# HGRN2 levels: q and k scaled in place by running products of the decays, in place of cumulated logarithms, differences and exponentials

## Chip, core and metric

The kernel runs on one core of one Trainium2 chip. The metric is device time in microseconds (us) of one execution, as the median of several runs. The engines are TensorE (PE; PEld is its weight load), VectorE (DVE), ScalarE (ACT), GpSimd (POOL) and SyncE (SP, which issues the weight DMAs).

## What is computed

Three blocks run over 256 tokens with a model width of 1024: a convolution and gated-delta layer, an HGRN2 layer, and a second block of attention heads and an MLP. The change lies in the HGRN2 layer, of 16 heads of width 128:

```
f = lower_bound + (1 - lower_bound) * sigmoid(f_raw);  q = silu(q_raw);  k = 1 - f
S_t = diag(f_t) S_{t-1} + k_t v_t^T;   o_t = S_t^T q_t
```

Written out, o_t is a sum over s <= t of v_s times the dot product of q_t and k_s, each channel weighted by the product of f over (s, t]. That product is what the change computes in another way.

## The kernel before

**Staging.** All tensors lie with the channel on the partition and the tokens along the free axis. The 16 heads are done in four groups g of HG = 4 heads, so q, k and f of a group are 128 x 1024 elements each (4 heads x 256 tokens). Weights come as slabs of 128 x 2048 words into a ring of six buffers RAW. ACT rounds each slab to WH (L1355; a ring of three), DVE writes the remainder WL (L1783): the steps `split:k:i`. ACT may start split k once PE has used slab k-3. Each projection of the odd layer is one slab, done by PE in two halves, `first:name` and `name`: f, q1 and z1 with 24 matmuls of 256 columns per half, the values i with 12 of 512 columns per half. Slabs 50 to 53 are f:1:0, f:1:1, z1:0:0, z1:0:1; 58 and 59 are f:2:0 and f:2:1; 60 to 63 are z1:1:0, z1:1:1, q1:2:0, q1:2:1; 66 and 67 are f:3:0 and f:3:1; 74 to 78 are z1:3:0, z1:3:1 and the first three of out:1.

**The levels.** Within a chunk of 128 tokens, the pairs (s, t) are divided into NL = 7 levels by the block size s = 1, 2, 4, ..., 64: at a level, t lies in the second half of a block of 2s tokens and s in its first half. For each group:

- `hf` takes the logarithm of f (ACT L1578) and cumulates it along the tokens (DVE L2060, eight scans).
- `hx(i)` subtracts from the cumulated logarithms the value at the middle of each block (DVE L2087, 1024 elements), and takes exponentials of both halves (ACT L1586, L1587).
- `hy(i)` multiplies q's second halves and k's first halves by them into a tile HX of two halves, one for even and one for odd i (DVE L2104, L2105, 512 elements each).
- `hd` and `hm(i)` are 8 matmuls of 128 x 128 each on PE (16 instructions in the trace, "PS<-layer ... x16"): `hd` is k against q as they are, `hm(i)` is HX against itself.
- `hd` on DVE masks the diagonal into HA (L2069), `hp(i)` copies the entries of level i into HA (L2110).
- `hc` is the product between the two chunks, `ho` the output against the values, `hr` the root mean square: two wide matmuls on PE, the root on ACT (L1365, L1366, L1371), and five operations on DVE (L1750 to L1752, L1794, L1795). `hr(g)` reads the banks that `hm(g+1, 0)` writes, and `hm(g+1, 0)` waits for it.

**Order.** Every engine runs its steps in an order written out by hand (ORDER_T for PE, ORDER_S for ACT, ORDER_V for DVE), one after the other, each waiting on semaphores for what it needs. On PE the projections stand between the `hm` steps. ACT loads another table whenever the function set changes (L1718). Before the change, `hy(i)` waits for `hm(i-2)` (the same half of HX). In the stretch at group 2 DVE's order before is `hy:2:0 hx:2:2 split:66:73 hz:1 hr:1:0 split:67:74 hy:2:1 hy:2:2 hd:2 hx:2:3`.

Of the kernel before, what the change touches and what calls it, by code (L numbers as in the profile page):

```python
# [487 lines left out]
gu:1:4:1 gu:1:5:0 gp:1:5:1 gp:1:6:0 gu:1:5:1 gu:1:6:0 gp:1:6:1 gv:1:0 gu:1:6:1 gs:1 gks:1 gv:1:1 go:1 gr:1:0 gr:1:1
pl:0:0 first:out:0:0:3 first:out:0:1:3 out:0:0:3 out:0:1:3 xt:0:0:0 pl:0:1 xt:0:0:1 ada:0:0 ada:0:1 ada:1:0 ada:1:1
xt:0:1:0 adat:0 first:gate:0:0:0 xt:0:1:1 first:gate:0:0:1 gate:0:0:0 gate:0:0:1 first:gate:0:1:0 adat:1 xt:1:0  # L490
xt:1:1 first:gate:0:1:1 gate:0:1:0 gate:0:1:1 ada:2:0 ada:2:1 xt:1:3 xt:1:2 first:f:0:0 adat:2 f:0:0 first:f:0:1
f:0:1 first:q1:0:0 q1:0:0 first:q1:0:1 q1:0:1 first:i:0:0 hd:0 i:0:0 hm:0:0 first:i:0:1 hm:0:1 i:0:1 first:f:1:0
# [5 lines left out]
hc:2 first:q1:3:1 ho:2 q1:3:1 hr:2:0 first:i:3:0 hd:3 i:3:0 first:i:3:1 i:3:1 hm:3:0 first:z1:3:0 hm:3:1 z1:3:0
hm:3:2 first:z1:3:1 hm:3:3 z1:3:1 ada:3:0 hm:3:5 ada:3:1 hm:3:4 out:1:0:0 adat:3 hm:3:6 out:1:1:0 hc:3 out:1:0:1
ho:3 out:1:1:1 hr:3:0 out:1:0:2 hr:3:1 out:1:1:2 pl:1:0 first:out:1:0:3 first:out:1:1:3 out:1:0:3 out:1:1:3 xt:2:0:0  # L500
pl:1:1 ada:8:0 xt:2:0:1 ada:8:1 ada:6:0 xt:2:1:0 ada:6:1 adat:8 xt:2:1:1 first:gate:1:0:0 first:gate:1:0:1
gate:1:0:0 gate:1:0:1 first:gate:1:1:0 adat:6 first:gate:1:1:1 gate:1:1:0 gate:1:1:1 ada:7:0 ada:7:1 ada:9:0 ada:9:1
# [1954 lines left out]
```

## Time and profile before

| | |
|---|---|
| median of 3 runs | 1143.58 us (1139.33 to 1143.73) |
| profiled execution | span 1137.7 us; no time of its own is listed beside it |
| PE busy | 1094.5 us (96%) |
| DVE busy | 810.0 us (71%) |
| ACT busy | 605.5 us (53%), of it 91.1 us for 71 table loads |
| chain that ended last | PE 83%, DVE 7%, ACT 6% |

The chain is followed back from the last instruction. A PE matmul's modelled end overlaps the next one's start, so whether PE lost time is read from the starts.

### The profile page before, as it was taken

How to read it: one execution, taken by the hardware profiler on the slowest of the kernel's cores; microseconds unless marked ns; L12 is line 12 of the kernel's file. 1: busy time of each engine (PE TensorE's matmuls, PEld its weight loads, DVE VectorE, ACT ScalarE, POOL GpSimd, SP SyncE). 2: the span in 40 equal slices, each digit the busy share in tenths (PEclk: the TensorE clock that was granted, in tenths of full speed). 3: DMA queues.
4: the chain of work that ended last, by engine and by line, in shares of the span. 5: the costliest groups of instructions: out<-in, count | busy, mean ns of one | idle time of the engine just before them, and what ended most of it. 6: DMA issues, size and time to landing. Idle time of an engine off the chain costs nothing.

```text
span 1137.7 us, 18770 instructions
## 1 busy us (share of the span) xinstructions
PE 1094.5 (96%) x7612; PEld 982.5 (86%) x7612; DVE 810.0 (71%) x1104; ACT 605.5 (53%) x675; POOL 13.0 (1%) x13
## 2 busy tenths in 40 slices
...
GB/s 326 169 181 145 122 110 112 114 147 185 112 38 116 254 256 118 146 148 112 136 124 122 139 185 185 259 288 208 141 154 176 18 204 185 179 181 179 169 213 19
DMA packets 26292, 181.30 MB, mean 159 GB/s; under 512 B 3040, under 2 KB 3296, under 8 KB 4960
## 3 DMA queue, kind: packets, MB, share of 16 engines
...
q10 hardware_dynamic: 1152, 5.45, 1.2%
q8 instruction: 62, 1.02, 0.4%
q14 instruction: 22, 0.18, 0.0%
...
## 4 chain that ended last, share of the span: by engine, by line
PE 83%; DVE 7%; ACT 6%; issue 2%; DMA 1%; POOL 0%; ACTq 0%; SPq 0%; DVEq 0%; POOLq 0%
PE PS L917 81%; DVE WL L1783 2%; ACT WH L1355 2%; ACT L1718 1%; DMA layer<-xt 1%; PE PS L1278 1%; DVE PS L1751 0%; DVE YL L1795 0%; DMA RAW<-wst 0%; PE PS L1140 0%; DVE layer_ln L2110 0%; POOL layer L2340 0%; DVE layer L2087 0%; ACT layer L1365 0%; ACT layer L1366 0%
## 5 line engine op out<-in xcount | busy, mean ns | idle before, releaser
L917 PE MATMUL PS<-XTH,WH 128*128 128x256 f32 x1392 | 405.6, 291 | 3.8 <-DVE XTL L1999 3.8
L1783 DVE TENSOR_TENSOR WL<-RAW,WH 128x2048 fp32r<-128x2048 f32 x138 | 316.7, 2295 | 111.1 <-ACT WH L1355 108.7
L917 PE MATMUL PS<-XTL,WH 128*128 128x256 f32 x1392 | 395.7, 284 | 0.0
L917 PE MATMUL PS<-XTH,WL 128*128 128x256 f32 x1392 | 395.6, 284 | 0.0
L1355 ACT ACTIVATE WH<-RAW 128x2048 fp32r<-128x2048 f32 x138 | 262.6, 1903 | 229.4 <-PE PS L917 225.5
L917 PEld LDWEIGHTS PS<-XTH,WH 128*128 128x128 f32 x1392 | 269.2, 193 | 7.0 <-ACT XTH L1508 4.6
L917 PEld LDWEIGHTS PS<-XTL,WH 128*128 128x128 f32 x1392 | 269.2, 193 | 2.4 <-issue 2.4
L917 PEld LDWEIGHTS PS<-XTH,WL 128*128 128x128 f32 x1392 | 268.8, 193 | 0.0
L917 PE MATMUL PS<-WH,YH 128*128 128x512 f32 x224 | 89.9, 401 | 3.7 <-DVE YL L1795 2.6
L1718 ACT ACT_TABLE_LOAD x71 | 91.1, 1283 | 1.7 <-ACT norms L1516 0.3
L917 PE MATMUL PS<-WH,YL 128*128 128x512 f32 x224 | 87.4, 390 | 0.0
L917 PE MATMUL PS<-WL,YH 128*128 128x512 f32 x224 | 87.2, 389 | 0.0
L917 PE MATMUL PS<-layer 128*128 128x128 f32 x640 | 80.7, 277 | 2.4 <-ACT layer L1562 1.1
L917 PEld LDWEIGHTS PS<-layer 128*128 128x128 f32 x640 | 76.9, 193 | 5.6 <-issue 2.3
L917 PE MATMUL PS<-WH,XTH 128*128 128x512 f32 x160 | 66.2, 414 | 3.6 <-DVE WL L1783 2.7
L917 PE MATMUL PS<-WH,XTL 128*128 128x512 f32 x160 | 63.1, 394 | 0.0
L917 PE MATMUL PS<-WL,XTH 128*128 128x512 f32 x160 | 62.8, 393 | 0.0
L917 PEld LDWEIGHTS PS<-WH,YH 128*128 128x128 f32 x224 | 42.1, 188 | 14.1 <-DVE YL L1795 3.8
L917 PEld LDWEIGHTS PS<-WH,YL 128*128 128x128 f32 x224 | 42.0, 188 | 9.0
L917 PEld LDWEIGHTS PS<-WL,YH 128*128 128x128 f32 x224 | 42.1, 188 | 8.9 <-issue 0.7
L917 PE MATMUL PS<-layer_x,layer 128*128 128x128 f32 x352 | 45.5, 275 | 0.3
L917 PEld LDWEIGHTS PS<-layer_x,layer 128*128 128x128 f32 x352 | 42.5, 192 | 1.1 <-DVE layer_x L1910 0.8
...
## 6 DMA issues: line engine op xcount, KB each, us to landing
...
```

The source lines that it names most:

```text
L917: return pe.matmul(o, lhsT, rhs, start=start, stop=stop)
L1278: last = pe.transpose(PS[:, 2, j * P:(j + 1) * P], SC[:, h % 2, j * P:(j + 1) * P], ident)
L1355: fn(WH[:, k % SPLIT_RING, 0:n], RAW[:, i % RAW_RING, 0:n], ACT.Copy).then_inc(scalar_done, 1)
L1718: act.preload_act_table_set(wanted)
L1783: tt(WL[:, i % RAW_RING, 0:n], RAW[:, i % RAW_RING, 0:n], as_float(WH[:, k % SPLIT_RING, 0:n]), ALU.subtract).then_inc(vector_done, 1)
```

## The change

`hf` and `hx` go, and with them the logarithms, scans, differences, exponentials and the tiles HB, HE and HX. `hy(g, 0)` multiplies q by f in place after `hd`. `hy(g, i)` for i from 1 to 6 waits for `hm(g, i-1)`, then multiplies q's second halves and k's first halves in place by the running product of each block (two operations of 512 elements), and last merges neighbouring products in place (512 elements at i = 1, 256 at i = 2, down to 16 at i = 6). `hy(g, 7)` scales two halves of 256 elements. The matmuls of `hm` and `hc` read HK and HQ. FS (the products) has two buffers; HS has a tile of its own. The orders of ACT and DVE are written anew; on PE, `hm:0:2`, `hm:1:5` and `hm:3:4` move ahead of `hm:0:3`, `hm:1:6` and `hm:3:5`.

```diff
--- before.py
+++ after.py
...
@@ -331,32 +331,24 @@
         for i in range(NL):
             out.append((later(step, "hm", g, i, on="T", banks=(0, 1) if i % 2 else (2, 3), readers="V",
                               read_in=("hp", g, i)), 1.0))
+            out.append((later(step, "hy", g, i + 1, on="V"), 0.0))
             if i:
                 out.append((later(step, "hp", g, i - 1, on="V"), 0.0))
-            if i + 2 <= NL:
-                out.append((later(step, "hx", g, i + 2, on="VS"), 0.0))
-            out.append((later(step, "hy", g, i + 1, on="V"), 0.0))
         more = g + 1 < HGRN_GROUPS
         out += [(later(step, "hp", g, NL - 1, on="V"), 0.0)]
-        if more:
-            out += [(later(step, "hf", g + 1, on="SV"), 0.0),
-                    (later(step, "hx", g + 1, 0, on="VS"), 0.0)]
         out += [(later(step, "hc", g, on="TS", banks=(2,)), 0.7),
                 (later(step, "ho", g, on="T", banks=(0, 1), readers="S",
                        read_in=("hq", g, pieces(g, HGRN_GROUPS)[-1][0])), 1.0)]
         out += [(later(step, "hq", g, p, on="S"), 0.0) for p, _ in pieces(g, HGRN_GROUPS)]
         out += [(later(step, "hz", g, on="V"), 0.0)]
         if more:
-            out += start(g + 1)[2:]
+            out += start(g + 1)
         out += [(later(step, "hr", g, p, on="TSV", banks=[2 + i for i in pairs], readers="V"), 1.0)
                 for p, pairs in pieces(g, HGRN_GROUPS)]
         return out
 
     def start(g):
-        return [(later(step, "hf", g, on="SV"), 1.0),
-                (later(step, "hx", g, 0, on="VS"), 0.0),
-                (later(step, "hd", g, on="TV", banks=(0, 1)), 1.0),
-                (later(step, "hx", g, 1, on="VS"), 0.0),
+        return [(later(step, "hd", g, on="TV", banks=(0, 1)), 1.0),
                 (later(step, "hy", g, 0, on="V"), 0.0)]
...
+first:q1:0:0 q1:0:0 first:q1:0:1 q1:0:1 first:i:0:0 hd:0 i:0:0 hm:0:0 first:i:0:1 hm:0:1 i:0:1 first:f:1:0 hm:0:2
+f:1:0 hm:0:3 first:f:1:1 f:1:1 hm:0:4 first:z1:0:0 hm:0:5 z1:0:0 hm:0:6 first:z1:0:1 z1:0:1 hc:0 first:q1:1:0 q1:1:0
+first:q1:1:1 ho:0 q1:1:1 hr:0:0 first:i:1:0 hd:1 i:1:0 first:i:1:1 i:1:1 hm:1:0 first:f:2:0 hm:1:1 f:2:0 first:f:2:1
+hm:1:2 f:2:1 hm:1:3 first:z1:1:0 hm:1:4 z1:1:0 first:z1:1:1 hm:1:5 z1:1:1 hm:1:6 first:q1:2:0 q1:2:0 first:q1:2:1 hc:1
+q1:2:1 ho:1 first:i:2:0 hr:1:0 i:2:0 hd:2 first:i:2:1 i:2:1 hm:2:0 first:f:3:0 f:3:0 hm:2:1 first:f:3:1 hm:2:2 f:3:1
+hm:2:3 first:z1:2:0 hm:2:4 z1:2:0 hm:2:5 first:z1:2:1 z1:2:1 first:q1:3:0 hm:2:6 q1:3:0 hc:2 first:q1:3:1 ho:2 q1:3:1
+hr:2:0 first:i:3:0 hd:3 i:3:0 first:i:3:1 i:3:1 hm:3:0 first:z1:3:0 hm:3:1 z1:3:0 hm:3:2 first:z1:3:1 hm:3:3 z1:3:1
+ada:3:0 hm:3:4 ada:3:1 hm:3:5 out:1:0:0 adat:3 hm:3:6 out:1:1:0 hc:3 out:1:0:1 ho:3 out:1:1:1 hr:3:0 out:1:0:2 hr:3:1
...
+adat:2 f:0:0 split:47:54 f:0:1 split:48:55 split:49:56 split:50:57 hd:0 hy:0:0 hy:0:1 hy:0:2 hp:0:0 split:51:58 hp:0:1
+hy:0:3 hy:0:4 hp:0:3 hp:0:2 split:52:59 f:1:0 split:53:60 hy:0:5 hp:0:4 split:54:61 hy:0:6 f:1:1 hy:0:7 hp:0:6 hp:0:5
+split:55:62 split:56:63 split:57:64 hz:0 split:58:65 hd:1 hy:1:0 hr:0:0 split:59:66 hy:1:1 hy:1:2 hp:1:1 hp:1:0
+split:60:67 hy:1:3 f:2:0 hp:1:2 split:61:68 hy:1:4 hy:1:5 hp:1:4 hp:1:3 split:62:69 f:2:1 split:63:70 hy:1:6 hy:1:7
+hp:1:6 hp:1:5 split:64:71 split:65:72 split:66:73 hz:1 hr:1:0 split:67:74 hd:2 hy:2:0 hy:2:1 hp:2:0 hy:2:2 split:68:75
+hp:2:1 hy:2:3 hp:2:2 split:69:76 hy:2:4 hp:2:3 f:3:1 hy:2:5 split:70:77 hp:2:4 hy:2:6 hp:2:5 split:71:78 f:3:0
+split:72:79 hy:2:7 hp:2:6 split:73:80 hz:2 split:74:81 hd:3 hy:3:0 hr:2:0 split:75:82 hy:3:1 hy:3:2 hp:3:1 hp:3:0
+hy:3:3 hp:3:2 split:77:86 hy:3:4 split:76:85 hp:3:3 hy:3:5 split:78:87 hy:3:6 hp:3:5 hp:3:4 adat:3 mod:0 split:79:88
...
         A1 = Arena("layer1")
         HK, HQ = A1.take(2 * HG, T), A1.take(2 * HG, T)
         HV = A1.take(2, NT, HG * P)
-        HB, HZ = A1.take(HG, T), A1.take(HG, T)
-        FS = A1.take(HG, T)
-        HE, HX = A1.take(2 * HG, T), A1.take(2 * HG, T)
+        HZ, HS = A1.take(HG, T), A1.take(HG, T)
+        FS = A1.take(2 * HG, T)
+        A1.take(3 * 4 * T)
         LBV, OML, LT1, LT2 = A1.take(16), A1.take(16), A1.take(32), A1.take(16)
         AL1 = Arena("layer1_ln", ln_at, 2 * D)
         HA, HC = AL1.take(8, P), AL1.take(HG, P)
         HOT = A1.take(HG, T)
-        HS = HX[:, HG:2 * HG, :]
+        RF = tiles(FS, 0, HG)
 
 
         A2 = Arena("block2")
...
             def t_hm(step, g, i):
                 pe.wait_ge(vector_done, vector_at("hy", g, i))
-                pe.wait_ge(vector_done, vector_at("hy", g, i))
                 for c in range(NT):
                     for h in range(HG):
-                        x = HX[:, i % 2 * HG + h, c * P:(c + 1) * P]
-                        last = mm(PS[:, step.banks[c], h * P:(h + 1) * P], x, x)
+                        m, s = g % 2 * HG + h, slice(c * P, (c + 1) * P)
+                        last = mm(PS[:, step.banks[c], h * P:(h + 1) * P], HK[:, m, s], HQ[:, m, s])
                 last.then_inc(tensor_done, 1)
 
             def t_hc(step, g):
                 pe.wait_ge(vector_done, vector_at("hy", g, NL))
-                pe.wait_ge(vector_done, vector_at("hy", g, NL))
                 for h in range(HG):
-                    x = HX[:, NL % 2 * HG + h, :]
-                    last = mm(PS[:, 2, h * P:(h + 1) * P], x[:, 0:P], x[:, P:T])
+                    m = g % 2 * HG + h
+                    last = mm(PS[:, 2, h * P:(h + 1) * P], HK[:, m, 0:P], HQ[:, m, P:T])
                 last.then_inc(tensor_done, 1)
 
             def t_ho(step, g):
...
-            def s_hx(g, i):
-                act.wait_ge(vector_done, vector_at("hx", g, i))
-                e = HE[:, i % 2 * HG:(i % 2 + 1) * HG, :]
-                if i < NL:
-                    s = LEVELS[i]
-                    blocks = flat(e).rearrange("p (b s) -> p b s", s=2 * s)
-                    fn(blocks[:, :, 0:s], blocks[:, :, 0:s], ACT.Exp, scale=-1.0)
-                    fn(blocks[:, :, s:2 * s], blocks[:, :, s:2 * s], ACT.Exp).then_inc(scalar_done, 1)
-                    return
-                fn(e[:, :, 0:P], e[:, :, 0:P], ACT.Exp, scale=-1.0)
-                fn(e[:, :, P:T], HB[:, :, P:T], ACT.Exp).then_inc(scalar_done, 1)
-
             def s_hc(g):
...
                 dve.wait_ge(scalar_done, scalar_at("f", g, p))
                 for a in range(2):
                     t, h = g * HG + 2 * p + a, 2 * p + a
-                    ts(FS[:, h, :], FS[:, h, :], OML[:, t:t + 1], LBV[:, t:t + 1], ALU.mult, ALU.add)
+                    f = FS[:, g % 2 * HG + h, :]
+                    ts(f, f, OML[:, t:t + 1], LBV[:, t:t + 1], ALU.mult, ALU.add)
                     k = HK[:, g % 2 * HG + h, :]
                     last = ts(k, k, OML[:, t:t + 1], None, ALU.mult)
                 last.then_inc(vector_done, 1)
 
-            def v_hf(g):
...
-                        s = slice(c * P, (c + 1) * P)
-                        last = dve.tensor_tensor_scan(HB[:, h, s], ONES[:], FS[:, h, s], 0.0,
-                                                      ALU.mult, ALU.add)
-                last.then_inc(vector_done, 1)
...
-            def v_hx(g, i):
-
-
-                if i >= 2:
-                    dve.wait_ge(vector_done, vector_at("hy", g, i - 2))
-                elif g:
-                    dve.wait_ge(vector_done, vector_at("hy", g - 1, NL - 1 + i))
-                b = HB
-                e = HE[:, i % 2 * HG:(i % 2 + 1) * HG, :]
+            def v_hy(g, i):
+
+                r = slice(g % 2 * HG, (g % 2 + 1) * HG)
+                q, k, f = HQ[:, r, :], HK[:, r, :], FS[:, r, :]
+                if i == 0:
+                    dve.wait_ge(tensor_done, tensor_at("hd", g))
+                    tt(q, q, f, ALU.mult).then_inc(vector_done, 1)
+                    return
+                dve.wait_ge(tensor_done, tensor_at("hm", g, i - 1))
+                s = LEVELS[i - 1]
+                x, z, y = (a.rearrange("p h (b s) -> p h b s", s=2 * s) for a in (q, k, f))
                 if i == NL:
-                    tt(e[:, :, 0:P], b[:, :, 0:P], b[:, :, P - 1:P].to_broadcast([P, HG, P]), ALU.subtract).then_inc(vector_done, 1)
+                    tt(x[:, :, 1, s:2 * s], x[:, :, 1, s:2 * s], y[:, :, 1, 0:1].to_broadcast([P, HG, s]), ALU.mult)
+                    tt(z[:, :, 0, 0:s], z[:, :, 0, 0:s], y[:, :, 0, s:s + 1].to_broadcast([P, HG, s]),
+                       ALU.mult).then_inc(vector_done, 1)
                     return
-                s = LEVELS[i]
+                x, z, y = (flat(a).rearrange("p (b s) -> p b s", s=2 * s) for a in (q, k, f))
                 n = HG * T // (2 * s)
-                b3 = flat(b).rearrange("p (b s) -> p b s", s=2 * s)
-                e3 = flat(e).rearrange("p (b s) -> p b s", s=2 * s)
-                tt(e3, b3, b3[:, :, s - 1:s].to_broadcast([P, n, 2 * s]), ALU.subtract).then_inc(vector_done, 1)
-
-            def v_hy(g, i):
-                dve.wait_ge(scalar_done, scalar_at("hx", g, i))
-                dve.wait_ge(scalar_done, scalar_at("q1", g, 1))
-                if i >= 2:
-                    dve.wait_ge(tensor_done, tensor_at("hm", g, i - 2))
-                elif i == 0 and g:
-                    dve.wait_ge(tensor_done, tensor_at("hm", g - 1, NL - 1))
-                r = slice(i % 2 * HG, (i % 2 + 1) * HG)
-                q, k = (a[:, g % 2 * HG:(g % 2 + 1) * HG, :] for a in (HQ, HK))
-                if i == NL:
-                    tt(HX[:, r, P:T], q[:, :, P:T], HE[:, r, P:T], ALU.mult)
-                    tt(HX[:, r, 0:P], k[:, :, 0:P], HE[:, r, 0:P], ALU.mult).then_inc(vector_done, 1)
-                    return
-                s = LEVELS[i]
-                x, e, y, z = (flat(a).rearrange("p (b s) -> p b s", s=2 * s) for a in (HX[:, r, :], HE[:, r, :], q, k))
-                tt(x[:, :, s:2 * s], y[:, :, s:2 * s], e[:, :, s:2 * s], ALU.mult)
-                tt(x[:, :, 0:s], z[:, :, 0:s], e[:, :, 0:s], ALU.mult).then_inc(vector_done, 1)
+                tt(x[:, :, s:2 * s], x[:, :, s:2 * s], y[:, :, 0:1].to_broadcast([P, n, s]), ALU.mult)
+                link(tt(z[:, :, 0:s], z[:, :, 0:s], y[:, :, s:s + 1].to_broadcast([P, n, s]), ALU.mult))
+                tt(y[:, :, 0:1], y[:, :, 0:1], y[:, :, s:s + 1], ALU.mult).then_inc(vector_done, 1)
...
```

## Rows read from the trace of the kernel before

**Rows 1.** Stretch, length; busy PE, PEld, DVE, ACT, POOL; granted clock, DMA share, GB/s.

```profile
430.00:703.00 273.00, 271.45 (x1967) 251.88 (x1966) 225.80 (x237) 191.52 (x193) 0.00 (x0) 1.00 0.39 139
```

**Rows 2.** Who PE waited for, 428 to 703 us (total, times, longest).

```profile
PE PS L917 <- ACT layer L1562: 1.1, 1, 1.1
PE PS L917 <- DVE layer_ln L2110: 0.5, 1, 0.5
```

**Rows 3.** Groups by line, 428 to 703 us (busy us, mean ns; idle before).

```profile
L1718 ACT ACT_TABLE_LOAD x34 | 43.6, 1283 | 0.7
L2087 DVE TENSOR_TENSOR layer<-layer 128x1024 f32<-128x1024 f32 x26 | 31.9, 1225 | 1.2
...
L2104 DVE TENSOR_TENSOR layer<-layer 128x512 f32<-128x512 f32 x28 | 19.4, 693 | 5.5 <-ACT layer L1562 4.6
```

**Rows 4.** Timeline of DVE, 566 to 577 us (start, duration).

```profile
566.31 1.23 DVE L1750 SCALAR_TENSOR_TENSOR layer<-layer 128x1024 f32<-128x1024 f32 x1 [3.49 <-ACT R L1371]
...
570.70 1.23 DVE L1795 TENSOR_TENSOR YL<-layer,YH 128x1024 fp32r<-128x1024 f32 x1
571.96 2.29 DVE L1783 TENSOR_TENSOR WL<-RAW,WH 128x2048 fp32r<-128x2048 f32 x1
574.28 0.69 DVE L2104 TENSOR_TENSOR layer<-layer 128x512 f32<-128x512 f32 x1
574.89 0.69 DVE L2105 TENSOR_TENSOR layer<-layer 128x512 f32<-128x512 f32 x1
...
576.94 1.22 DVE L2069 TENSOR_TENSOR layer_ln<-PS,CST 128x1024 f32<-128x1024 f32 x1
```

**Rows 5.** Timeline of PE (start, time to the modelled end), nine places.

```profile
497.58 1.95 PE L917 MATMUL PS<-layer 128*128 128x128 f32 x16
499.28 0.48 PE L917 MATMUL PS<-WH,XTH 128*128 128x512 f32 x1
...
507.58 1.95 PE L917 MATMUL PS<-layer 128*128 128x128 f32 x16
...
565.38 1.95 PE L917 MATMUL PS<-layer 128*128 128x128 f32 x16
...
572.66 1.95 PE L917 MATMUL PS<-layer 128*128 128x128 f32 x16
...
642.50 1.95 PE L917 MATMUL PS<-layer 128*128 128x128 f32 x16
...
647.16 1.95 PE L917 MATMUL PS<-layer 128*128 128x128 f32 x16
...
656.57 1.06 PE L917 MATMUL PS<-RAW,SCZ 128*32 128x512 f32 x8
658.09 2.02 PE L917 MATMUL PS<-layer 128*128 128x128 f32 x16 [0.45 <-DVE layer_ln L2110]
```

**Rows 6.** Timeline of DVE at three other places.

```profile
412.51 0.41 DVE L2047 TENSOR_SCALAR layer<-layer 128x256 f32<-128x256 f32 x1 [2.10 <-ACT layer L1554]
...
413.42 0.34 DVE L2049 TENSOR_SCALAR layer<-layer 128x256 f32<-128x256 f32 x1
...
499.62 1.23 DVE L2069 TENSOR_TENSOR layer_ln<-PS,CST 128x1024 f32<-128x1024 f32 x1 [0.51 <-PE PS L917]
...
657.27 0.72 DVE L2110 COPY_PREDICATED layer_ln<-CST,PS 128x512 f32<-128x512 uint32 x1
```

**Rows 7.** The same view as rows 1, of five later stretches.

```profile
770.00:775.00 5.00, 5.00 (x25) 5.00 (x25) 2.46 (x2) 1.08 (x1) 0.00 (x0) 0.50 1.02 419
775.00:780.00 5.00, 5.00 (x25) 5.00 (x25) 2.83 (x4) 0.38 (x2) 0.00 (x0) 0.50 0.41 169
...
940.00:945.00 5.00, 1.22 (x6) 0.42 (x5) 4.83 (x8) 4.79 (x9) 0.00 (x0) 0.94 0.91 380
945.00:950.00 5.00, 5.00 (x31) 5.00 (x32) 4.25 (x4) 2.78 (x2) 0.00 (x0) 0.72 0.00 0
950.00:955.00 5.00, 5.00 (x44) 5.00 (x44) 1.42 (x4) 2.30 (x2) 0.00 (x0) 1.00 0.32 92
```

More of the change, by code:

```diff
@@ L383, in plan @@
         u()
-    interleave(start(0), values(0))
+    interleave([(lambda: None, 1.0)] + start(0), values(0))
     for g in range(HGRN_GROUPS):
@@ L488 @@
[L488 to L492, printed above, removed]
@@ L498 @@
[L498 to L502, printed above, removed]
@@ L513 @@
-down:1:2 down:1:3 down:1:4 first:down:1:5 down:1:5
+first:az:1:0 go:0 az:1:0 gr:0:0 first:ab:1:0 ab:1:0 first:zb:1:0 zb:1:0 gc:1 first:zb:1:1 zb:1:1 first:ah:1:1 norm:q:1
+ah:1:1 vtr:1 first:ac:1:1 ac:1:1 gk:1 first:az:1:1 gkk:1 az:1:1 first:ab:1:1 gp:1:0:1 gp:1:0:0 ab:1:1 gu:1:0:1
+gu:1:0:0 out:0:0:0 gp:1:1:1 gp:1:1:0 out:0:1:0 gu:1:1:0 gu:1:1:1 gp:1:2:0 out:0:0:1 gu:1:2:0 gp:1:2:1 out:0:1:1
+gp:1:3:0 gu:1:2:1 gu:1:3:0 out:0:0:2 gp:1:4:0 gp:1:3:1 out:0:1:2 gu:1:3:1 gu:1:4:0 gp:1:4:1 gp:1:5:0 gu:1:4:1 gu:1:5:0
@@ new lines @@
+turn:8 pv:6 score:11 pv:7 score:12 turn:9 pv:8 turn:10 pv:9 score:13 mln turn:11 pv:10 score:15 pv:11 turn:12 score:14
+pv:12 out2:0:0 turn:13 out2:1:0 pv:13 turn:14 turn:15 pv:14 pv:15 first:out2:0:1 first:out2:1:1 out2:0:1 out2:1:1
+ada:10:0 ada:10:1 ada:11:0 adat:10 ada:11:1 xt:5:3 xt:5:1 xt:5:0 xt:5:2 adat:11 ff:0 ff:1 ff:2 ff:3 ff:4 ff:5 ff:6
+ff:7 ff:8 ff:9 ff:10 ff:11 ff:12 ff:13 ff:14 ff:15 ff:16 ff:17 ff:18 ff:19 ff:20 ff:21 down:0:0 down:0:1 down:0:2
+down:0:3 down:0:4 first:down:0:5 down:0:5 down:1:0 down:1:1 down:1:2 down:1:3 down:1:4 first:down:1:5 down:1:5
@@ new lines @@
+hq:3:1 hq:3:0 split:82:91 hr:3:0 split:83:92 hr:3:1 pl:1:0 lna:1:0 xt:2:0:0 lna:1:1 pl:1:1 xt:2:0:1 split:84:98
+ada:8:1 xt:2:1:0 ada:6:1 xt:2:1:1 split:85:99 split:86:100 first:gate:1:0:1 rms:0:0:0 split:87:101 gate:1:0:1
+rms:0:1:0 first:gate:1:1:1 rms:0:0:1 gate:1:1:1 rms:0:1:1 ada:7:1 xt:4:2 xt:4:0 ada:9:1 xt:4:1 xt:4:3 ada:4:1
+split:88:108 split:89:109 ga gb split:90:110 feat:8 split:91:111 qn:1:2 feat:0 split:92:112 qn:0:0 feat:1 split:93:113
+qn:0:1 feat:2 split:94:114 qn:0:2 split:95:115 feat:3 split:96:116 feat:5 split:97:117 feat:4 feat:6 split:98:118
@@ new lines @@
+gu:1:2:0 split:37:37 gp:1:2:1 gp:1:3:0 split:38:38 gu:1:2:1 gu:1:3:0 gp:1:4:0 gp:1:3:1 split:39:39 gu:1:3:1 gu:1:4:0
+gp:1:4:1 gp:1:5:0 gu:1:4:1 gu:1:5:0 gp:1:5:1 gp:1:6:0 gu:1:5:1 gu:1:6:0 gp:1:6:1 gu:1:6:1 lb gks:1 lb2 gz:1 gr:1:0
+gr:1:1 first:out:0:0:3 first:out:0:1:3 lna:0:0 lnb:0:0:0 out:0:0:3 lnb:0:0:1 out:0:1:3 lna:0:1 xt:0:0:0 lnb:0:1:0
+split:40:45 xt:0:1:0 xt:0:0:1 lnb:0:1:1 split:41:46 xt:0:1:1 adat:0 split:42:47 first:gate:0:0:1 split:43:48
+gate:0:0:1 adat:1 first:gate:0:1:1 split:44:51 xtl:1:0 gate:0:1:1 xtl:1:1 split:45:52 xtl:1:2 xtl:1:3 split:46:53
```

164 lines of the change are left out of this document (60 added, 104 removed).

## Prediction

> **What bounds the kernel now.** I read the page first: PE is busy 96% of the span and carries 83% of the chain that ended last, so a change off PE counts only where PE waits for it. Then the windows by stage: over the whole HGRN2 stretch, 430 to 703 us, PE is busy 271.45 of 273 us at granted clock 1.00 (2.4 GHz), DVE 225.8, ACT 191.5 [rows 1]. Then PE's waits there: two, 1.1 us for ACT's silu of q1 and 0.5 us for a copy of DVE [rows 2]. So at most 1.6 us of waiting can be won, some 2.1 us with the refill of PE behind each (a block of 16 takes 1.70 us to the next start, 497.58 to 499.28 [rows 5], 1.95 us after a wait: 658.09 to the next small matmul, 0.25 more). Last I read the timelines of PE and DVE for the latencies: DVE starts 0.34 us after PE has begun the next block (499.28 to 499.62), and PE starts 0.10 us after DVE's last operation (657.27 + 0.72 to 658.09) [rows 5, 6].
>
> **What is removed, and what it is worth.** 28 differences of 1.225 us (34 us) and the scans leave DVE; 25 table switches (by the ACT orders, 37 before and 12 after, from f:0:0 on) of 1.283 us each (32 us) and the exponentials leave ACT [rows 3]. None of it stands in PE's order, so it is worth only the two waits of [rows 2]. The first, before `hd:0`, is ACT: q1:0:1 stands behind `hx:0:0`, `hx:0:1` and two table loads, which go. It is won: -1.25. The second goes too, but another takes its place (F below). PE's matmuls stay the same in number and shape.
>
> **What is added.** Before, `hy(i)` waited for `hm(i-2)`; now for `hm(i-1)`, since PE reads the very tiles that it overwrites. So between two `hm` on PE there must pass, counted from the first's end: 0.34, the two multiplications (574.28 to 574.89 + 0.69: 1.30 [rows 4]), 0.03, the merge, and 0.10. The trace has no merge. From 1225 ns for 1024 elements and 693 for 512 [rows 3], an element is 1.04 ns and the fixed part 0.16 us: I take 0.69, 0.43, 0.29, 0.23, 0.19 and 0.18 us for i = 1 to 6. If striding over short blocks cost nothing and everything ran like a fixed part, the bound below would be 0.16; the bound above, 0.69 for each, adds up to 0.5 us at late levels. The nearest rows, differences over all block sizes at one mean of 1.225, say that strides cost nothing, so I keep the line. The need is 2.46 us at i = 1 and 1.96 at i = 5.
>
> PE's cover is one half projection: 4.66 between `hm` starts less 1.70, 2.96 us (642.50 to 647.16 [rows 5]). So a lone chain fits. It doesn't fit where DVE has a split (2.29 [rows 4]), an `f` (four operations, 412.51 to 413.76, 1.25) or an `hp` (0.72) [rows 6] left over when `hm` ends. I walked DVE's new order against PE's, group by group, T being the end of an `hm`. Each stop costs its lateness plus 0.25.
>
> - **A, `hm:0:0`.** Cover: the second half of i:0:0, (572.66 - 565.38 - 1.70)/2 = 2.8 [rows 5]. Need: 0.34 + the mask 1.22 + `hy:0:0` 1.23 + 0.04 + 0.10 = 2.9, and split 50 ends some 0.3 into it. +0.64.
> - **B, `hm:0:5`**, T after `hm:0:3`. DVE: `hy:0:4` 1.9 (latency in), two `hp` 1.5, split 52 2.3, f:1:0 1.3, split 53 2.35, `hy:0:5` 1.55, 0.1, so 11.05. PE: 5.84 + 1.70 + 2.96 = 10.50. +0.80.
> - **C, `hm:1:4`**, T after `hm:1:2`: `hy:1:3` 2.0, f:2:0 1.3, `hp` 0.75, split 61 2.3, `hy:1:4` 1.6, 0.1, so 8.05 against 2.95 + 1.71 + 2.96 = 7.62. +0.67.
> - **D, `hm:1:6`**, T after `hm:1:4`: `hy:1:5` 1.9, two `hp` 1.5, split 62 2.3, f:2:1 1.3, split 63 2.35, `hy:1:6` 1.55, 0.1, so 11.0 against 10.5. +0.75.
> - **E, `hm:2:0`.** The large one. DVE's new order is `hr:1:0 split:67:74 hd:2 hy:2:0`; before, `hy:2:0` stood ahead of `hr:1:0` and `hd:2` later. `hr:1:0` can't start before 566.31, where it waited for ACT's root, and ends at 571.93; split 67 ends at 574.25 [rows 4]. Then come the mask 1.22 and `hy:2:0` 1.23 with gaps of 0.04: 576.77, and PE at 576.87. PE is ready at 572.66 [rows 5]. The root itself waits for PE's own `hr`, so nothing removed makes it earlier. 4.2 + 0.25 = +4.45. Everything behind (`hm:2:0` and all projections) stands still.
> - **F, `hm:3:5`.** Between `hm:3:4` and `hm:3:5` PE has only eight small matmuls, 1.0 us (656.57 [rows 5]), against a need of 1.97: 0.97 + 0.25. From 656.57 to the projection behind, the sum is 6.64 where the trace took 6.28 with its own wait. +0.36.
> - **G, H, `hm:1:0` and `hm:3:0`.** `hr:0:0` now stands behind `hd:1` and `hy:1:0`, and `hm:1:0` claims the banks that it reads. 499.62 + 1.23 + 0.03 + 1.23 + 0.03 + 5.62 (rows 4: 566.31 to 571.93) + 0.10 = 507.86 against 507.58 [rows 5, 6]. +0.5; group 3 has the same order, +0.5.
>
> All the other intervals come out with cover to spare, two (`hm:1:1`, `hm:3:1`) within 0.5 us. The sum of A to H is 8.67; less 1.25, **+7.4 us**.
>
> **The clock.** PE was down to 1.22 busy us of 5 with its last wait 940 to 945, and behind it the granted clock is 0.72, that is a part at 1.2 GHz: 31 matmuls ran where the next 5 us had 44 [rows 7], 13 x 0.114 = 1.5 us. Stop E is of that size, after PE had been full. I add 1.5 for it; without the clock's fall it is nothing. The Trainium skill, TensorE: Matmul & The Clock Gate (HAM oscillation), says that waits between bursts of matmuls let the clock fall and that the next burst starts cold; by that the sum is 8.9, without it 7.4.
>
> So the profiled execution, span 1137.7, would take 1146.6, a ratio of 1.0078. The shown median, 1143.58, is 5.9 above the span (1.6 for the fastest run); the ratio applied to it gives 1152.5, the difference 1152.5 too. I say **1152 us**.
>
> **Rivals.**
>
> 1. *Only E binds.* A, B, C, D, G and H are differences of 0.1 to 0.6 us between chains of up to 11 us; if DVE's small operations are a little cheaper (merges at 0.16), they vanish, and PE's refills with them: 1143.6 - 1.25 + 4.45 + 0.36 = 1147.2. For it: small margins. Against: they add up from measured durations.
> 2. *The other side: PE never waits for the new chains.* Place: the order around `hd:2`. If DVE got through `hr:1:0`, the split, the mask and `hy:2:0` by 572.6, which takes 4.2 us off (the root earlier, or the mask not behind it), the relief of DVE and ACT would be all that is left: 1143.6 - 2.1 = 1141.5, no change that can be measured. It decides at E below some 1 us. Against it: [rows 4] has each duration.
> 3. *The clock stays low for longer.* From 770 to 780 it is 0.50 throughout, with PE busy [rows 7]: 10 us at 1.2 GHz, which can cost up to half, 5 us. If E brought that instead of 1.5: 1152.5 + 3.5 = 1156.
> 4. *Faster through the clock.* That same stretch, 770 to 780, could run at 2.4 GHz when all behind HGRN2 is shifted, and win up to 5 us. With rival 2 or 1: 1136.5 to 1142. The windows show nothing that would trigger it.
>
> **How the numbers follow.** Some 0.5% (5.7 us; the runs shown spread over 0.4%) is what a measurement of this kernel can tell from no change: up to 1149.3 is the same. Forecast 0.55 (1149 to 1155; 0.03 of it under the bound), rival 1 0.15, rival 2 0.12, rival 3 0.10, rival 4 0.08. Slower: 0.52 + 0.10 = 0.62. Same: 0.03 + 0.15 + 0.12 = 0.30. Faster 0.08. The range 1142 to 1156 holds the forecast, rival 1, half of rival 2 and half of rival 3; what is left out is some 0.19; the bounds of the merge (at most +0.5 us at each of the few tight places) lie in it.
>
> **What would show it.** In the changed kernel's trace: 12 table loads where 37 were; no wait of PE at `hd:0`; PE's longest wait in the stretch on DVE's `hy:2:0`, some 4.2 us, with a mask and a 1024-element product just before it; five or so waits of 0.2 to 0.6 us on the merge (one of 1.0 at `hm:3:5`); granted clock under 1 just behind the long wait; DVE some 35 us less busy (34 and the scans, less 8 of merges), ACT more than 32. The prediction is wrong if PE waits elsewhere than at these places, if merges take more than 0.7 us, or if the time differs outside HGRN2.

## The result, and the profile after

| | median | runs |
|---|---|---|
| before | 1142.12 us | 4, 1139.33 to 1143.73 |
| changed | 1155.17 us | 4, 1151.65 to 1158.24 |

The ratio is 1.0112 (95% interval 1.0094 to 1.013): slower, by 13 us. The forecast was 1152 us (1142 to 1156) and slower with 0.62; the measured time lies inside the range, 0.8 us below its upper bound. All ratios here are taken over the fast runs, so they are not quite the quotients of the medians, and one execution of 1292 us (before, beside again) and one of 1219 us (repaired2) are left out of them. The profiled execution of the changed kernel took 1154.55 us. Its page (span; busy time by engine; the chain that ended last):

```profile
span 1152.7 us, 18510 instructions
...
PE 1101.0 (96%) x7612; PEld 986.5 (86%) x7612; DVE 769.4 (67%) x1060; ACT 531.4 (46%) x582; POOL 13.0 (1%) x13
...
PE 80%; DVE 12%; ACT 5%; issue 1%; DMA 1%; POOL 0%; ACTq 0%; SPq 0%; DVEq 0%; POOLq 0%
```

DVE is 40.6 us less busy than before (810.0) and ACT 74.1 (605.5), with 46 table loads in the span; the span is 15.0 us longer. The work was taken off DVE and ACT as forecast, but it wasn't on the path.

A wait of PE that moves the start of its next block is called a stop below, and the matmuls that PE has to do before it needs the awaited value are its cover. I measure the HGRN2 stretch from one landmark on PE to another: from the start of the 512-wide matmuls at 380 us to the start of the projection behind `hm:3:5`. Before it is 380.03 to 662.85, 282.82 us; in the changed kernel 380.12 to 673.40, 293.28 us: +10.5. What lies behind it took 474.85 us before and 479.30 after: +4.5. The second part turned out not to be the change's (below).

Who PE waited for inside the stretch, 428 to 715 us (total, times, longest), where [rows 2] had two waits of 1.6 us in all:

```profile
PE PS L903 <- DVE layer L2028: 4.4, 2, 4.0
PE PS L903 <- DVE layer L2042: 2.1, 4, 0.8
PE PS L903 <- DVE layer_ln L2047: 2.0, 1, 2.0
```

L2028 is `hy(g, 0)`, L2042 the merge, L2047 `hp`. The first wait of [rows 2] is gone, the rest is new. The place of the longest on DVE (start, duration), answering to [rows 4]:

```profile
567.96 1.23 DVE L1712 SCALAR_TENSOR_TENSOR layer<-layer 128x1024 f32<-128x1024 f32 x1 [4.24 <-ACT R L1355]
...
573.61 2.29 DVE L1745 TENSOR_TENSOR WL<-RAW,WH 128x2048 fp32r<-128x2048 f32 x1
575.94 1.23 DVE L2020 TENSOR_TENSOR layer_ln<-PS,CST 128x1024 f32<-128x1024 f32 x1
577.20 1.23 DVE L2028 TENSOR_TENSOR layer<-layer 128x1024 f32<-128x1024 f32 x1
```

and on PE, with the next projection, answering to the row at 572.66 of [rows 5]:

```profile
578.57 3.38 PE L903 MATMUL PS<-layer 128*128 128x128 f32 x16 [4.04 <-DVE layer L2028]
581.71 0.36 PE L903 MATMUL PS<-XTH,WH 128*128 128x256 f32 x1
```

`hr:1:0` began only when ACT's root came, split 67 (L1745), the mask and `hy:2:0` followed without a gap, and PE began 0.14 us after the last of them. The block then took 3.14 us to the next start where it takes 1.70: the windows (busy time by engine, granted clock last but two) show the granted clock under 1.00, that is at its lower level for a part of the time:

```profile
575.00:580.00 5.00, 1.43 (x7) 1.46 (x8) 3.35 (x3) 3.84 (x3) 0.00 (x0) 0.80 0.58 213
580.00:585.00 5.00, 5.00 (x38) 5.00 (x38) 2.87 (x4) 0.00 (x0) 0.00 (x0) 0.86 0.00 0
```

The prediction had not foreseen the wait of 1.97 us at `hm:3:2`. This is DVE ahead of `hm:3:2`:

```profile
652.55 0.69 DVE L2040 TENSOR_TENSOR layer<-layer 128x512 f32<-128x512 f32 x1 [2.50 <-PE PS L903]
653.16 0.68 DVE L2041 TENSOR_TENSOR layer<-layer 128x512 f32<-128x512 f32 x1
653.88 0.64 DVE L2042 TENSOR_TENSOR layer<-layer 128x256 f32<-128x256 f32 x1
654.55 2.63 DVE L2047 COPY_PREDICATED layer_ln<-CST,PS 128x512 f32<-128x512 uint32 x2
```

and PE, from `hm:3:1` to `hm:3:2`:

```profile
650.50 1.95 PE L903 MATMUL PS<-layer 128*128 128x128 f32 x16
...
657.28 2.02 PE L903 MATMUL PS<-layer 128*128 128x128 f32 x16 [1.97 <-DVE layer_ln L2047]
```

The product and the merge, `hy:3:2`, are done at 654.52; PE waits for `hp:3:0`, the second of the two copies. `hm:3:2` writes the banks that `hm:3:0` wrote, and these are free only when `hp:3:0` has read them.

The new operations by size (busy us, mean ns):

```profile
L2047 DVE COPY_PREDICATED layer_ln<-CST,PS 128x512 f32<-128x512 uint32 x28 | 25.0, 894 | 1.0
...
L2042 DVE TENSOR_TENSOR layer<-layer 128x512 f32<-128x512 f32 x4 | 2.8, 695 | 0.1
L2042 DVE TENSOR_TENSOR layer<-layer 128x256 f32<-128x256 f32 x4 | 2.5, 632 | 0.1
L2042 DVE TENSOR_TENSOR layer<-layer 128x128 f32<-128x128 f32 x4 | 1.6, 408 | 0.1
L2042 DVE TENSOR_TENSOR layer<-layer 128x64 f32<-128x64 f32 x4 | 1.1, 274 | 0.1
```

The merges of 256 and 128 elements cost nearly half as much again as my line gave (0.43 and 0.29). The table has each of the stretch's differences, from the starts of the `hm` blocks in the two traces (for A to D, from the first start behind each block, which takes in the slower refill of PE there):

| step | forecast | measured |
|---|---|---|
| wait before `hd:0` | -1.25 | -1.25 |
| A, B, C, D | +0.64, 0.80, 0.67, 0.75 | +0.62, 0.70, 0.71, 0.63 |
| E, `hm:2:0` | +4.45 | +4.19 |
| clock behind E | +1.5 | +1.44 |
| F, `hm:3:5` | +0.36 | +0.35 |
| G, H | +0.5, +0.5 | +0.27, +0.29 |
| `hm:2:3` | 0 | +0.31 |
| `hm:3:2` | 0 | +2.12 |
| sum | +8.9 | +10.4 (landmarks: +10.5) |

### The profile page after: what moved, and what is told of

It reads as the page before. It is cut to its first block, busy times and chain, and to the rows that moved or that the text cites. A ratio compares the mean times of both kernels' runs of the same rounds, so it can differ in the third digit from the quotient of the medians.

```text
span 1152.7 us, 18510 instructions
## 1 busy us (share of the span) xinstructions
PE 1101.0 (96%) x7612; PEld 986.5 (86%) x7612; DVE 769.4 (67%) x1060; ACT 531.4 (46%) x582; POOL 13.0 (1%) x13
## 3 DMA queue, kind: packets, MB, share of 16 engines
q10 hardware_dynamic: 1152, 5.45, 1.2%
## 4 chain that ended last, share of the span: by engine, by line
PE 80%; DVE 12%; ACT 5%; issue 1%; DMA 1%; POOL 0%; ACTq 0%; SPq 0%; DVEq 0%; POOLq 0%
PE PS L903 79%; DVE WL L1745 3%; ACT WH L1339 1%; DVE YL L1757 1%; DVE PS L1713 1%; DVE layer_ln L2047 1%; DMA layer<-xt 1%; DVE layer L2040 1%; DVE layer L2041 1%; PE PS L1262 1%; ACT L1680 1%; DVE layer_ln L2020 0%; DVE layer L1714 0%; DVE layer L2028 0%; DVE layer L1712 0%
## 5 line engine op out<-in xcount | busy, mean ns | idle before, releaser
L1745 DVE TENSOR_TENSOR WL<-RAW,WH 128x2048 fp32r<-128x2048 f32 x138 | 316.7, 2295 | 132.2 <-ACT WH L1339 129.7
```

Of the source, the lines that this page charges most:

```text
L1745: tt(WL[:, i % RAW_RING, 0:n], RAW[:, i % RAW_RING, 0:n], as_float(WH[:, k % SPLIT_RING, 0:n]), ALU.subtract).then_inc(vector_done, 1)
```

## The experiments

The theory: the in-place products as such cost nothing, since PE's cover holds them; the time is lost where hand-written orders leave DVE work between a block of PE and the `hy` or `hp` that the next one needs, and in the clock behind the largest such stop. The rivals: the tighter dependence (`hy(i)` behind `hm(i-1)`) costs time whatever the order; and, for the 4.5 us behind the stretch, that the change makes them.

**again.** The changed kernel itself.

> The changed kernel itself once more. From PE's start on the gate projection at 380 us to the first out:1 projection behind hm:3:5 the kernel before took 282.8 us and the changed one 293.3 us; outside that stretch the changed profile is longer by 4.5 us. If the stops between hm steps are what the change costs (theory), the stretch is 293.3 again within 0.5 us, with the same waits of PE (4.0 at hm:2:0, 2.0 at hm:3:2). If the 4.5 us outside come from where the granted clock happens to fall (theory), they differ from this profile by 1 us or more, with the falls at other places; if they are the change's own doing (rival), they are 4.5 again within 0.5, with the falls at 742 and 913 us again.

The median is 1156.61 us against 1143.27 for before, the ratio 1.0118 (1.0102 to 1.0134). The waits are the same to 0.01 us at `hm:2:0` and `hm:3:2` (4.04 and 1.97), but the stretch took 296.1 us, not 293.3 within 0.5 as expected: the clock was low for longer behind the first wait, and fell behind the second too. Windows of this run:

```profile
575.00:580.00 5.00, 2.20 (x10) 2.23 (x11) 2.58 (x3) 3.10 (x2) 0.00 (x0) 0.66 0.50 200
580.00:585.00 5.00, 5.00 (x31) 5.00 (x30) 3.27 (x4) 0.00 (x0) 0.00 (x0) 0.66 0.00 0
...
655.00:660.00 5.00, 3.03 (x21) 2.86 (x20) 2.61 (x2) 3.79 (x3) 0.00 (x0) 0.85 0.63 210
660.00:665.00 5.00, 5.00 (x37) 5.00 (x37) 3.99 (x5) 0.00 (x0) 0.00 (x0) 0.81 0.01 3
```

So one profile doesn't fix the price of a clock fall. Behind the stretch the kernel took 479.48 us once more, which looked like the change's own doing until the kernel before was looked at again.

**before_look.** The kernel before itself.

> The kernel before itself once more. The profile shown of it has a span of 1137.7 us, near its fastest run; behind the HGRN2 stretch it took 474.85 us, where five kernels with the new levels took 479.2 to 481.8 with falls of the granted clock near 742 and 913 us that this profile lacks. Theory (the profile shown of before was a lucky one, the change does nothing behind the stretch): a second profile of before takes 478 to 481 us behind the stretch, with those falls, and some 282.8 in the stretch. Rival (the new levels cost 4.5 us later on): 474.9 again within 0.5, without those falls.

The median is 1143.55 us against 1142.95 for the same kernel (ratio 1.0008, 0.9998 to 1.0018). The stretch took 282.75 us, and what lies behind it 479.45, not 474.85. This is a window behind the stretch in the first profile of before, at granted clock 1.00:

```profile
905.00:910.00 5.00, 5.00 (x25) 4.14 (x24) 0.64 (x4) 1.63 (x1) 0.00 (x0) 1.00 0.16 28
```

The same place in before_look:

```profile
900.00:905.00 5.00, 3.54 (x14) 2.33 (x13) 4.09 (x12) 1.69 (x6) 0.00 (x0) 0.69 0.01 3
905.00:910.00 5.00, 5.00 (x15) 3.92 (x15) 0.71 (x3) 0.11 (x2) 0.00 (x0) 0.62 0.00 0
```

and in the changed kernel, some 11 us later:

```profile
910.00:915.00 5.00, 3.54 (x17) 2.48 (x16) 4.20 (x12) 1.61 (x6) 0.00 (x0) 0.75 0.01 3
915.00:920.00 5.00, 5.00 (x16) 3.76 (x15) 1.40 (x4) 0.99 (x4) 0.00 (x0) 0.57 0.00 0
```

The unchanged kernel shows the same two falls of the clock (here and near 731 us) and the same 479.4 us. The first profile was of an execution without them. The new levels have both kinds too: the profile of repaired2 (below) has the clock at 1.00 at both places, and 474.9 us behind the stretch.

```profile
905.00:910.00 5.00, 5.00 (x25) 4.12 (x24) 1.75 (x5) 3.05 (x6) 0.00 (x0) 1.00 0.42 133
```

So no run shows the change doing anything behind HGRN2; against before's second profile the span grows by 10.7 us, 10.5 of it in the stretch.

**split_later.** One step moved on DVE:

```diff
-... hr:1:0 split:67:74 hd:2 hy:2:0 hy:2:1 ...
+... hr:1:0 hd:2 hy:2:0 split:67:74 hy:2:1 ...
```

> Only DVE's order differs: split:67:74 stands behind hd:2 and hy:2:0, not ahead of them. Theory (the stop at hm:2:0 is the length of DVE's chain hr:1:0, split, mask, hy:2:0): the wait goes from 4.04 to 1.75 us, that is by one split of 2.29, and the stretch from 380 on from 293.3 to 291.0 us; to 289.6 if the clock's fall behind the wait goes with it. Rival (PE waits there for ACT's values or for the banks, not for DVE's order): the wait stays at 4.0 and the stretch at 293.3.

The median is 1149.94 us, the ratio 1.0068 (1.0055 to 1.0081). The stretch is 289.63 us and the clock stays at 1.00 in both windows from 575 to 585. PE:

```profile
575.31 2.02 PE L903 MATMUL PS<-layer 128*128 128x128 f32 x16 [1.72 <-DVE layer L2028]
577.09 0.37 PE L903 MATMUL PS<-XTH,WH 128*128 128x256 f32 x1
```

Of the wait 2.32 us go, the length of one split (2.29), and 1.3 us more with the clock. The median falls by 5.2 us.

**cover_only.** The same place from PE's side, DVE's order as in the changed kernel:

```diff
-... i:2:1 hm:2:0 first:f:3:0 f:3:0 hm:2:1 ...
+... i:2:1 first:f:3:0 hm:2:0 f:3:0 hm:2:1 ...
```

> The changed kernel with one move in PE's order: the first half of f:3:0 ahead of hm:2:0. Theory (PE's wait there is DVE's chain less PE's cover): the wait goes from 4.04 to 1.08 us, by the 2.96 of one half projection, and the clock keeps 2.4 GHz behind it; hy:2:1 and its merge (2.0 us) then fit under the other half. Rival (the wait is moved, not covered): PE waits 2.9 us more in all at hm:2:1 and behind.

There is one execution, of 1149.05 us; the stretch is 288.98 us. PE:

```profile
577.84 2.02 PE L903 MATMUL PS<-layer 128*128 128x128 f32 x16 [1.17 <-DVE layer L2028]
```

Half a projection put ahead of the block takes 2.87 us off the wait, its own length (2.96) but for 0.09, and the clock stays at 1.00 there. DVE's chain is as late as ever: a stop is that chain less what PE has to do meanwhile.

**hp_first.** The unforeseen stop:

```diff
-... split:75:82 hy:3:1 hy:3:2 hp:3:1 hp:3:0 ...
+... split:75:82 hy:3:1 hp:3:0 hy:3:2 hp:3:1 ...
```

> Only DVE's order differs: hp:3:0 stands ahead of hy:3:2, hp:3:1 behind it. Theory (hm:3:2 claims the banks that hp:3:0 reads, and hp:3:0 stood behind hy:3:2 and hp:3:1, 2.03 + 1.32 + 1.32 us): PE's wait of 1.97 us at hm:3:2 goes to nothing, the stretch from 380 on goes from 293.3 to 291.2 us. Rival (hm:3:2 is late because of hy:3:2's own merge and strides): the wait stays above 1 us.

The median is 1152.12 us, the ratio 1.0081 (1.0068 to 1.0094). PE's wait at `hm:3:2` is gone: its block begins at 655.16, 4.65 us after the last. On DVE:

```profile
649.35 0.69 DVE L2042 TENSOR_TENSOR layer<-layer 128x512 f32<-128x512 f32 x1
650.08 1.32 DVE L2047 COPY_PREDICATED layer_ln<-CST,PS 128x512 f32<-128x512 uint32 x1
652.56 0.69 DVE L2040 TENSOR_TENSOR layer<-layer 128x512 f32<-128x512 f32 x1 [1.17 <-PE PS L903]
...
658.99 0.71 DVE L2047 COPY_PREDICATED layer_ln<-CST,PS 128x512 f32<-128x512 uint32 x1
```

The copy now lies in DVE's idle time. The stretch is 292.26 us, 1.1 more than expected; the clock was low around `hm:2:0` for as long as in again (0.60 and 0.71 in the windows from 575 to 585), and against that run's 296.1 the stretch is 3.8 us shorter.

**repaired.** All stops mended by order alone, the operations of the changed kernel untouched. The core of it:

```diff
-split:49:56 split:50:57 hd:0 hy:0:0 hy:0:1
+split:49:56 hd:0 hy:0:0 split:50:57 hy:0:1
-hp:0:3 hp:0:2 split:52:59 f:1:0 split:53:60 hy:0:5 hp:0:4 split:54:61 hy:0:6 f:1:1 hy:0:7
+hp:0:2 hp:0:3 split:52:59 f:1:0 hy:0:5 split:53:60 hp:0:4 hy:0:6 f:1:1 split:54:61 hy:0:7
-hr:0:0 split:59:66 hy:1:1
+hr:0:0 hy:1:1 split:59:66
-hp:1:2 split:61:68 hy:1:4 hy:1:5 hp:1:4 hp:1:3 split:62:69 f:2:1 split:63:70 hy:1:6
+hp:1:2 hy:1:4 split:61:68 hp:1:3 hy:1:5 hp:1:4 split:62:69 f:2:1 hy:1:6 split:63:70
-hp:3:2 split:77:86 hy:3:4 split:76:85 hp:3:3 hy:3:5 split:78:87
+hp:3:2 hy:3:4 split:77:86 hp:3:3 hy:3:5 split:76:85 split:78:87
 # on PE, beside cover_only's edit:
-ada:3:0 hm:3:4 ada:3:1 hm:3:5
+hm:3:4 ada:3:0 ada:3:1 hm:3:5
```

with the edits of split_later and hp_first.

> All arithmetic as in the changed kernel; only orders differ: at each of PE's stops the split (or f) ahead of the awaited hy or hp stands behind it, hm:2:0 has one half projection more ahead of it, and ada:3:0 stands behind hm:3:4. Theory (all of the stretch's loss is DVE's order, none of it the in-place products as such): left are some 0.3 us each at hm:1:0 and hm:3:0; the stretch from 380 on takes 282.8 - 1.25 (q1) - 0.5 (the old wait at 658) + 0.6 = 281.7 us, and the whole 1141 us, no different from before within 0.3%. Rival (a chain without two buffers can't be hidden whatever the order): the stretch stays above 287 us and the whole is slower than before by 0.5% or more.

The median is 1143.57 us against 1143.27, the ratio 1.0002 (0.9989 to 1.0014): the whole loss is gone. The stretch is 282.54 us (281.7 expected), as long as before's, and from `hd:0` on PE waits in it once, at its end, for a split:

```profile
658.56 2.02 PE L903 MATMUL PS<-layer 128*128 128x128 f32 x16
661.00 0.47 PE L903 MATMUL PS<-WH,YH 128*128 128x512 f32 x1 [0.41 <-DVE WL L1745]
```

The rival that the tighter dependence costs time in any order falls: 282.54 us is far from the 287 and more that it asked for.

**repaired2 and repaired3.** Does anything remain to be won? repaired2 gives `hm:1:0` cover on PE, and moves `hp:1:0`, `hp:2:1`, split 59 and two splits of group 3 on DVE; repaired3 puts one more split behind an `hy`:

```diff
-hy:2:2 split:68:75 hp:2:1 hy:2:3 hp:2:2 split:69:76 hy:2:4
+hy:2:2 hp:2:1 hy:2:3 split:68:75 hp:2:2 split:69:76 hy:2:4
 # repaired3
-hp:2:2 split:69:76 hy:2:4
+hp:2:2 hy:2:4 split:69:76
```

> The repaired orders with three more moves: hm:1:0 and hm:1:1 one half projection later with hp:1:0 ahead of hy:1:2, split:68:75 behind hy:2:3, and split:76:85 ahead of split:77:86, whose lateness cost 0.4 us in the first repair. Theory: the stretch from 380 on goes from 282.5 to 281.5 us (0.35 at hm:1:0, 0.3 at hm:2:3, 0.4 at out:1:0:0), 1.3 less than before. That is 0.1%: the whole is the same as before, perhaps 1 us less. Rival: each move only shifts the stop to the next hm, and the stretch stays at 282.5.

> The second repair with the place mended that it broke: in the second repair hy:2:4 stood behind two splits, and PE waited 1.49 us for it at hm:2:4. Here split:69:76 stands behind hy:2:4. Theory: that wait goes with its refill, the stretch from 380 on takes 283.1 - 1.6 = 281.5 us (282.8 in the kernel before), the whole is 1.2 us under the kernel before, 0.998 to 0.999 of it, and nothing below that is to be had by orders, since PE then has no wait of more than 0.3 us left in the stretch. Rival: a further stop appears behind it, and the stretch stays at 283.

repaired2 has a median of 1140.81 us against 1142.95 and a ratio of 0.9989 (0.9974 to 1.0003); its stretch is 283.13 us, not the 281.5 expected. By moving split 68 I had put two splits around a copy ahead of `hy:2:4`, where PE had cover for one. DVE in repaired2:

```profile
585.64 0.41 DVE L2042 TENSOR_TENSOR layer<-layer 128x128 f32<-128x128 f32 x1
586.09 2.29 DVE L1745 TENSOR_TENSOR WL<-RAW,WH 128x2048 fp32r<-128x2048 f32 x1
588.41 0.72 DVE L2047 COPY_PREDICATED layer_ln<-CST,PS 128x512 f32<-128x512 uint32 x1
589.16 2.29 DVE L1745 TENSOR_TENSOR WL<-RAW,WH 128x2048 fp32r<-128x2048 f32 x1
```

and PE:

```profile
593.23 2.02 PE L903 MATMUL PS<-layer 128*128 128x128 f32 x16 [1.49 <-DVE layer L2042]
```

repaired3 has 1142.59 us against 1143.13 and a ratio of 0.9991 (0.9979 to 1.0002); its stretch is 282.11 us (281.5 expected), with one wait of 0.46 us left, on a merge. Neither can be told from before by its time. The waits of [rows 2] are 1.6 us, by the prediction's count 2.1 with refills, and the best of the three mended orders has 0.7 less in its profile (282.82 to 282.11).

**q1_first.** The kernel before, with its one larger wait taken away on ACT:

```diff
-... split:49:56 hx:0:0 hx:0:1 q1:0:1 split:50:57 ...
+... split:49:56 q1:0:1 hx:0:0 hx:0:1 split:50:57 ...
```

> The kernel before, with one move in ACT's order: q1:0:1 ahead of hx:0:0 and hx:0:1. Theory (the only thing that the relief of ACT is worth is PE's wait at hd:0): that wait of 1.1 us goes, PE's start of hd:0 comes 1.25 us earlier, and as hy:0:0 and hy:0:1 come later by some 0.6 us and a table load, no other wait appears. Rival: the later hx:0:0 delays hm:0:0, and the 1.25 us are lost again at once. The whole time can't tell either (0.1%); the profile can.

The median is 1143.33 us, the ratio 1.0 (0.9987 to 1.0013), the stretch 283.01 us. So here the rival came true: the 1.25 us at `hd:0` are won and given back behind it, most of it by `hc:0`, which starts 0.7 us later against the block before it than in the kernel before, since PE waits 0.53 us for a copy. The rest goes at the blocks between `hd:0` and 450 us. The wait was slack for DVE's chain.

**strides.** The changed kernel with added work in `hz:0` that nothing uses: a fill and eight products in place, 256, 128 or 512 elements with steps of 1, 2, 4 or 8 between them.

> The changed kernel with nine more DVE operations inside step hz:0, on a tile that nothing else uses: a memset and eight products, in this order 256 elements dense, 256 at a step of 2, 4 and 8 elements, 128 at 8 and 4, 512 at 2 and 4. In the trace the merges took 0.695 us for 512 elements (step 2), 0.632 for 256 (step 4), 0.408 for 128 (step 8), where the prediction had 0.69, 0.43 and 0.29. Theory (from a step of 4 elements on, an element costs about twice): 0.43, 0.43, 0.63, 0.63, 0.41, 0.41, 0.69, 1.1 us. Rival (the merges' surplus is a read of values that were just written, or the step grows the price further each time): 0.43 for all of 256, or more at 8 than at 4.

There is one execution, of 1158.4 us. The added work makes a new wait of PE, 5.06 us at `hm:1:0`, so its time says nothing of the change. The dense product and the sum of the seven strided ones on DVE:

```profile
493.89 0.43 DVE L2063 TENSOR_TENSOR layer<-layer 128x256 f32<-128x256 f32 x1
494.35 4.57 DVE L2065 TENSOR_TENSOR layer<-layer 128x256 f32<-128x256 f32 x7
```

and the seven in the view of their line (shortest, median and longest in ns):

```profile
L2065 DVE TENSOR_TENSOR layer<-layer x7: 399/631/1103, 494.4 to 497.8; 128x256 f32<-128x256 f32 x3, 128x128 f32<-128x128 f32 x2, 128x512 f32<-128x512 f32 x2
```

256 elements: 0.43 us dense, 0.42 at a step of 2, 0.68 and 0.63 at 4 and 8. 512 elements: 0.69 at a step of 2, 1.10 at 4. 128 elements: 0.40 and 0.43 at 4 and 8, where the line gives 0.29. A step of two elements is free. At four, an element costs some 1.6 ns against 1.04, as an estimate from the two sizes at that step ((1.10 - 0.68) / 256), and at eight about as much ((0.63 - 0.43) / 128). The rival that the merges' surplus comes from reading values just written falls, since the products at steps of 1 and 2 read such values as well.

## Why the prediction was right, and where it was wrong

**The bound, right.** PE's order sets the time; some 40 us off DVE and 74 off ACT, 32 of them table loads, were worth one wait of 1.25 us. q1_first shows that even this is no sure gain: in the kernel before it came back as other waits.

**E and the clock, right.** PE waited 4.04 us and its start moved by 4.19, for a forecast of 4.45; the clock's fall cost 1.44 with the refill in it, for 1.5. split_later and cover_only show the mechanism from either side, DVE's chain and PE's cover. By HAM oscillation (the Trainium skill, TensorE: Matmul & The Clock Gate), a wait between bursts lets the clock fall: the four profiles with the wait of 4.04 us agree (low for 3.4 us in the changed kernel and in strides, 6.8 in again, 6.9 in hp_first); those with 1.72 and 1.17 us at the same place show no fall. That is not a rule for every wait: of the five profiles with the wait of 1.97 us at `hm:3:2`, only again shows a fall behind it. My rival 3, longer at the low clock, was therefore part of the truth: in again the longer fall and the second one added 2.8 us to the stretch.

**A to D and F, right** to 0.12 us each, in part by luck. B's durations add up to 11.0, not 11.05. In F the errors cancel: from the first small matmuls to the projection behind, the changed kernel took 6.63 us for a forecast of 6.64, though the block `hm:3:4` took 1.98 us to the next start and not 1.70, and the one behind the stop 1.78 and not 1.95.

**The refill, mis-sized.** The prediction adds 0.25 us to every stop, from the block at 658.09 that takes 1.95 us to the small matmuls behind it. The changed kernel has a block in front of such matmuls without any wait, and it takes 1.98:

```profile
667.77 2.05 PE L903 MATMUL PS<-layer 128*128 128x128 f32 x16
669.75 1.06 PE L903 MATMUL PS<-RAW,SCZ 128*32 128x512 f32 x8
```

So the 0.25 goes with the small matmuls beside the block, and not with the wait. Ahead of a projection, a block takes 1.78 us behind a wait and mostly 1.70 without one (1.75 and 1.81 at two places in the kernel before), so a wait adds 0.08. That is why G and H measured 0.27 and 0.29 for 0.5, and E 4.19 for 4.45: the latenesses themselves (507.86 against 507.58, 4.2) were right.

**The rivals.** Rival 1 (the small stops vanish) and rival 2 (no stop at `hm:2:0`) are out, though repaired reaches rival 2's outcome, no measurable change, by another order; rival 4 didn't come.

**The step that failed** is "All the other intervals come out with cover to spare". The prediction named it as a sign of being wrong that PE waits elsewhere than at its places, and PE does. At `hm:3:2` PE has one half projection of cover and DVE needs, from 652.20, 0.35 + 1.33 + 0.64 + 2.63 + 0.1: 5.1 us. Two errors lie in it. I walked the chain only up to `hy`, and forgot that a block also claims the banks of the block two before it, which `hp` must have read; the order `hy:3:2 hp:3:1 hp:3:0` puts that copy last. And I took 0.72 us for every `hp`, from a row of a late level. Here, at the first two levels, two take 2.63, and the kernel before had shown as much, in its timeline of DVE:

```profile
516.36 2.69 DVE L2110 COPY_PREDICATED layer_ln<-CST,PS 128x512 f32<-128x512 uint32 x2
```

Without the claim on the banks there is no stop, since `hy:3:2` was done in time; with it and 0.72 us for each copy it would have been some 0.9 us (2.12 - 2.63 + 1.44). As it was, it cost 2.12 us.

**The merges, mis-sized.** They took 0.63 and 0.41 us for i = 2 and 3, where the line gave 0.43 and 0.29; strides shows that it is the step. The sum was touched little. They are one part of the reason for the other stop that wasn't foreseen, `hm:2:3` (+0.31). DVE worked without a gap from 589.59 us until 0.14 us before that block began, and these are three of its operations:

```profile
590.92 0.64 DVE L2042 TENSOR_TENSOR layer<-layer 128x256 f32<-128x256 f32 x1
...
593.92 1.32 DVE L2047 COPY_PREDICATED layer_ln<-CST,PS 128x512 f32<-128x512 uint32 x1
...
596.61 0.41 DVE L2042 TENSOR_TENSOR layer<-layer 128x128 f32<-128x128 f32 x1
```

The two merges took 0.33 us more than forecast, and the copy `hp:2:1` 0.60 more than 0.72. The start of `hm:2:3` was late by 0.30 (597.16 against 592.20 + 1.70 + 2.96), so by these durations neither surplus alone makes the stop; no run tests it.

**The total.** The forecast for the stretch was +8.9 us, the profile shows +10.5, and the median moved by 13. The 1152 us stood on a median of 1143.58, which the fourth run took to 1142.12. The clock behind the stops varies (again: 13.3 us of stretch), and so do the two falls behind HGRN2 in either kernel; how much of the remaining 2.5 us is due to each isn't shown, as four runs of each don't settle it. The first profile, of 1137.7 us, was an execution without those falls. That 1155 lies in the range is owed in part to its width: the forecast's own terms give 8.9 us, and the unforeseen 2.4 us at `hm:3:2` and `hm:2:3` and the varying clock came on top.
